# Further rows of each expert gathered as quarter rows and turned by one VectorE transpose, with a table of positions in 32-row blocks

## The chip, the core and the metric

The kernel runs on one core of a Trainium2 chip. The metric is the device time of one execution in microseconds (us), from three timed runs. A core has TensorE (PE in the profile, PEld for its weight loads), VectorE (DVE), ScalarE (ACT), GpSimd (POOL) and SyncE (SP, which here only issues DMAs). Each runs its own instruction stream in order; they meet at semaphores.

## The reference, cut to what matters

One decoder layer on 1024 tokens of width 1024: forgetting attention, layer norm, then a mixture of 64 experts of which each token picks 8, plus one shared expert, and a second layer norm. The part that matters here:

```python
scores = sigmoid(xf @ w_router); top_e = the 8 experts of a token; w = their weights
for each expert e, for the tokens that chose it:
    h  = silu(x @ w_gate[e]) * (x @ w_up[e])      # 1024 -> 256
    yb = (h @ w_down[e]) * w                       # 256 -> 1024
    acc[token] += yb
out = layer_norm(alpha * x + acc + shared(x))
```

How many tokens an expert gets depends on the data. The mean is 8 * 1024 / 64 = 128.

## The kernel before, in words

Attention takes the first part of the span. Then, tile by tile of 128 tokens, come the output projection, the first layer norm, the router, and `place`, in which VectorE works out for each of a token's 8 choices a slot in a table of positions in DRAM; POOL scatters the token numbers into it (`list_tokens`, eight indirect DMAs a tile, L635). The normed rows go to `rows_scratch` in DRAM, 1024 values and behind them the 64 routing weights, so that a row is 4352 bytes.

The expert stage runs the shared expert on eight tiles and then the 64 experts one after the other. Every expert takes its first 128 tokens as one block (POOL `gather`, L657: 128 whole rows into `x_rows`). If it has more, the rest goes in **further blocks** of 32 rows (`gather_further`, L670, into a buffer `x_rows2`). An expert has `nx` further blocks; on these inputs each has none or one.

TensorE works on 32-bit data as a high and a low part (`xb_hi`, `xb_lo` for rows, `gu_hi`, `gu_lo`, `dn_hi`, `dn_lo` for weights): ScalarE casts the high part, VectorE subtracts to get the low one. For each expert e, TensorE turns the hidden values of the expert before (`turn_h`, L1039), multiplies gate and up (`gate_up`, L1025, L1028, L1031), turns the rows of the next expert (`turn_next`, L1015), multiplies the expert before down (`down`, L1052 to L1060), and, if e has a further block, multiplies that (`gate_up_further`, L1084, L1085), whose 32 rows take high and low part side by side in `xo`. What is left of the further block is done one expert later: `turn_h_further` (L1093) and `down_further` (L1102, L1103).

The further block's rows have to be turned so that the width lies on the partitions. Before, TensorE does it in `turn_further` (L1074): eight transposes of 32 rows by 128 columns into half of a PSUM bank, between `turn_next` and `down`. ScalarE casts them to `xo` (`further_rows_hi`, L1486), VectorE subtracts (`further_rows_lo`, L1938), and TensorE's L1084 waits for that.

The order on VectorE within one expert is written out by hand in `expert` (L2008): low parts of weights (L1918), `h_of` (L1926), the last low part, `next_rows` (`xb_lo`, L1922, and the copy of the next expert's weights column, L1934), then, if the expert before had a further block, `further_y` (L1958), then `further_rows_lo` (L1938), then the low parts of the down weights. On POOL the order is: `gather` for the expert three ahead, `add_further`, `gather_further` for the expert two ahead, and `add_first` (L682), which adds a finished block into `sums_scratch` in DRAM. Each `add_first` waits until the one before has landed. POOL's instructions are strictly in this order, so what waits there holds up all that stands behind it.

The last expert's results don't go through DRAM but are placed by TensorE; the tiles are then summed, normed and stored.

Of the kernel before, what the change touches and what calls it, by code (L numbers as in the profile page):

```python
# [5 lines left out]
P = 128  # L6
BANK = 512
ALU = mybir.AluOpType
# [70 lines left out]
TAB_BLOCKS = 1 + (T - P) // XR  # L79
TAB = E * TAB_BLOCKS  # L80
ROWS = T + P
ROW_W = D + E
# [13 lines left out]
def build(nc, x, w_in, b_f, w_out, ln1_g, ln1_b, router, router_bias, w_gate, w_up, w_down, ws_gate, ws_up,  # L96
          ws_down, ln2_g, ln2_b, out):
    with ExitStack() as ctx:
# [18 lines left out]

        rows_dram = nc.dram_tensor("rows_scratch", (ROWS, ROW_W), F32, kind="Internal").ap()


        sums = [nc.dram_tensor(f"sums_scratch{i}", (ROWS, D), F32, kind="Internal").ap() for i in range(2)]
        tab_dram = nc.dram_tensor("tab_scratch", (P * TAB, 1), I32, kind="Internal").ap()
# [9 lines left out]
        with ExitStack() as early:  # L132
# [37 lines left out]
            with ExitStack() as d:  # L170
# [50 lines left out]
                pos_b = sb("pos_b", [P, E], c=d)  # L221
                pos_h = sb("pos_h", [P, E], c=d)
# [7 lines left out]
                tab0 = sb("tab0", [P, TAB], I32, c=d)  # L230
                zeros = sb("zeros", [P, ROW_W], c=d)
                nblk = [sb(f"nblk{i}", [1, E], c=d) for i in range(2)]
                nblk_i = [sb(f"nblk_i{i}", [1, E], I32, c=d) for i in range(2)]
        with ExitStack() as m:
# [3 lines left out]
            xg = [sb(f"x_rows{i}", [P, ROW_W], c=m) for i in range(3)]  # L238
# [4 lines left out]
            gu_x = sb("gu_x", [XR, 2 * FF], c=m)  # L243
# [8 lines left out]
            sidx = [sb(f"sidx{i}", [P, 1], I32, c=m) for i in range(3)]  # L252
            sb("to_64_bytes", [P, 8], c=m)
# [4 lines left out]
            tab = sb("tab", [P, TAB], I32, c=m)  # L258
# [121 lines left out]
        def _(sp):  # L380
# [89 lines left out]
            def tile(t):  # L470
# [4 lines left out]
                sp.dma_start(rows_dram[ds(t * P, P), 0:D], x1[:]).then_inc(S["x1_stored"], 16)  # L475
# [3 lines left out]
            def weights_out(t):  # L479
                sp.wait_ge(S["wts_ok"], t + 1)  # L480
                sp.dma_start(rows_dram[ds(t * P, P), D:ROW_W], wts[:]).then_inc(S["wts_stored"], 16)
# [30 lines left out]
            def load_rows(b):  # L512
                sp.dma_start(xg[b % 2][:, 0:D], rows_dram[b * P:(b + 1) * P, 0:D]).then_inc(rows_in[b % 2], 16)
# [32 lines left out]
            sp.wait_ge(S["c_fill"], 48)  # L546
            sp.wait_ge(S["extra_ok"], 2)
            sp.dma_start(tab[:], tab_dram.rearrange("(p n) o -> p (n o)", p=P)).then_inc(S["c_loads"], 16)
# [36 lines left out]
        def _(pool):  # L585
# [27 lines left out]
            g.iota(e8[:], pattern=[[TAB_BLOCKS, E]], base=1, channel_multiplier=0, allow_small_or_imprecise_dtypes=True).then_inc(S["c_const"], 1)  # L613
            g.iota(tok_all[:], pattern=[[P, TT]], base=0, channel_multiplier=1).then_inc(S["c_const"], 1)
            g.iota(tab0[:], pattern=[[0, TAB]], base=T, channel_multiplier=1).then_inc(S["c_const"], 1)
# [5 lines left out]
            pool.dma_start(tab_dram.rearrange("(p n) o -> p (n o)", p=P), tab0[:]).then_inc(S["c_fill"], 16)  # L621
            pool.dma_start(rows_dram[T:ROWS, :], zeros[:]).then_inc(S["c_fill"], 16)
            pool.dma_start(sums[0][T:ROWS, :], zeros[:, 0:D]).then_inc(S["c_fill"], 16)
            pool.dma_start(sums[1][T:ROWS, :], zeros[:, 0:D]).then_inc(sent[2], 16)
            pool.wait_ge(S["c_fill"], 48)
# [20 lines left out]
            def gather(i, e, count, free):  # L646


                if not (static(e) and e < 2):
                    pool.wait_ge(got[i], 8 * (e - i))  # L650
                stand(pool)
                g.tensor_copy(gidx[i][:], tab[:, ds(e * TAB_BLOCKS, 1)]).then_inc(idx_ok[i], 1)
                pool.wait_ge(idx_ok[i], count + 1)
                for s, value in free:
# [3 lines left out]
                                     in_offset=bass.IndirectOffsetOnAxis(ap=gidx[i][:, 0:1], axis=0)).then_inc(got[i], 16)  # L658

            def gather_further(par, e, k, x):  # L660

                if not static(x):
                    with pool.If(x > 0):
                        pool.wait_ge(S["x_in"], 16 * x)
# [1489 lines left out]
```

## Time and profile before

| what | value |
|---|---|
| three timed runs | 1650.76, 1644.61, 1645.97 us |
| their median | 1645.97 us |
| span of the profiled execution (first to last instruction) | 1640.5 us |
| median less that span | 5.5 us |
| PE busy, share of the span | 1578.0 us, 96% |
| DVE busy | 1182.3 us, 72% |
| ACT busy | 1032.5 us, 63% |
| POOL busy | 503.7 us, 31% |
| DMA, mean over the span | 225 GB/s |

The profile is one execution; of its time the records hold the span alone, and what lies around it is taken as the 5.5 us by which the median stands above it. A row of the timeline begins with the start and the duration in us; in square brackets stands how long the engine sat idle before it and who ended the wait. The profile's matmul durations overlap, since matmuls are pipelined: what one costs is read from start to start. A row of the groups has the line, engine, operation, tiles (out<-in), shapes and count, then busy us in total and mean ns of one, then idle us before and who ended it.

### The profile page before, as it was taken

How to read it: one execution, taken by the hardware profiler on the slowest of the kernel's cores; microseconds unless marked ns; L12 is line 12 of the kernel's file. 1: busy time of each engine (PE TensorE's matmuls, PEld its weight loads, DVE VectorE, ACT ScalarE, POOL GpSimd, SP SyncE). 2: the span in 40 equal slices, each digit the busy share in tenths (PEclk: the TensorE clock that was granted, in tenths of full speed). 3: DMA queues.
4: the chain of work that ended last, by engine and by line, in shares of the span. 5: the costliest groups of instructions: out<-in, count | busy, mean ns of one | idle time of the engine just before them, and what ended most of it. 6: DMA issues, size and time to landing. Idle time of an engine off the chain costs nothing.

```text
span 1640.5 us, 32188 instructions
## 1 busy us (share of the span) xinstructions
PE 1578.0 (96%) x8246; PEld 1310.0 (80%) x8247; DVE 1182.3 (72%) x2036; ACT 1032.5 (63%) x1706; POOL 503.7 (31%) x495
## 2 busy tenths in 40 slices
PE   6999999999999999899999999999999999999986
PEld 6897888888887788778878888888888888888863
DVE  4214777777777788847777787777876787888866
ACT  3214666666666655527677787666776777877854
POOL 0000000000000135432544454543454445454426
PEclk9999999999999999899999999999999999999995
DMA  7223222222123533657999999999999999999987
GB/s 245 91 81 91 72 48 68 58 65 71 45 71 103 170 134 138 227 196 281 337 291 318 305 357 367 326 289 264 334 318 288 274 353 331 342 368 370 367 252 282
DMA packets 161320, 368.63 MB, mean 225 GB/s; under 512 B 53009, under 2 KB 73489, under 8 KB 161265
## 3 DMA queue, kind: packets, MB, share of 16 engines
q1 hardware_dynamic: 136272, 284.21, 49.7%
q0 software_dynamic: 24992, 83.73, 19.7%
q8 instruction: 28, 0.46, 0.1%
q14 instruction: 28, 0.22, 0.0%
HBM read 294.39 MB, written 65.11 MB: 219 GB/s over the span
## 4 chain that ended last, share of the span: by engine, by line
PE 72%; DVE 8%; DMA 8%; issue 5%; ACT 3%; ACTq 2%; POOL 1%; SPq 0%; DVEq 0%; POOLq 0%
PE bank_pair L1025 6%; PE bank_pair L1031 6%; PE bank_pair L1028 6%; DMA sums_scratch<-ys,sidx 5%; PE q_ps L91 4%; PE q_ps L93 4%; PE q_ps L92 4%; PE out_ps L916 4%; PE k_ps L894 4%; PE out_ps L1084 3%; PE out_ps L1085 3%; PE q_ps L1015 3%; PE k_ps L1052 2%; PE k_ps L1053 2%; PE k_ps L1060 2%
## 5 line engine op out<-in xcount | busy, mean ns | idle before, releaser
L1918 DVE TENSOR_TENSOR gu_lo<-raw_gu,gu_hi 128x1024 fp32r<-128x1024 f32 x260 | 306.3, 1220 | 25.5 <-ACT gu_hi L1396 25.5
L1396 ACT CAST gu_hi<-raw_gu 128x1024 fp32r<-128x1024 f32 x260 | 253.2, 1050 | 2.3 <-DMA raw_gu<-in_moe_w_gate_dram 1.5
L1025 PE MATMUL bank_pair<-gu_hi,xb_hi 128*128 128x512 f32 x576 | 233.1, 405 | 5.5 <-DVE gu_lo L1918 4.2
L1028 PE MATMUL bank_pair<-gu_lo,xb_hi 128*128 128x512 f32 x576 | 226.9, 394 | 0.0
L682 POOL DMA_INDIRECT sums_scratch<-ys,sidx x63 | 122.1, 1939 | 148.9 <-DMA sums_scratch<-ys,sidx 116.0
L1918 DVE TENSOR_TENSOR dn_lo<-raw_dn,dn_hi 128x1024 fp32r<-128x1024 f32 x130 | 152.6, 1213 | 2.9 <-ACT dn_hi L1396 2.4
L1031 PE MATMUL bank_pair<-gu_hi,xb_lo 128*128 128x512 f32 x576 | 142.7, 390 | 2.0 <-DVE xb_lo L1922 2.0
L1301 ACT CAST pt_hi<-k_ps 128x512 fp32r<-128x512 f32 (+1 forms) x192 | 85.7, 482 | 75.4 <-PE k_ps L894 74.7
L1025 PEld LDWEIGHTS bank_pair<-gu_hi,xb_hi 128*128 128x128 f32 x576 | 110.1, 191 | 28.8 <-issue 6.4
L613 POOL IOTA e<- 128x64 f32 x1 | 0.2, 185 | 428.8 <-DVE xs L1714 428.8
L1396 ACT CAST dn_hi<-raw_dn 128x1024 fp32r<-128x1024 f32 x130 | 130.0, 1052 | 2.9 <-DMA raw_dn<-in_moe_w_down_dram 2.9
L1031 PEld LDWEIGHTS bank_pair<-gu_hi,xb_lo 128*128 128x128 f32 x576 | 108.0, 188 | 24.8 <-DVE xb_lo L1922 2.4
L1028 PEld LDWEIGHTS bank_pair<-gu_lo,xb_hi 128*128 128x128 f32 x576 | 109.7, 190 | 21.1
L657 POOL DMA_INDIRECT x_rows<-rows_scratch,gidx x64 | 77.4, 1210 | 154.2 <-DVE wcol L1934 122.6
L1692 DVE TENSOR_TENSOR pt_lo<-k_ps,pt_hi 128x512 fp32r<-128x512 f32 (+1 forms) x192 | 100.4, 551 | 27.8 <-ACT pt_hi L1301 27.0
L1052 PE MATMUL k_ps<-dn_hi,ht_hi 128*128 128x512 f32 x288 | 118.4, 411 | 0.0
L1053 PE MATMUL k_ps<-dn_lo,ht_hi 128*128 128x512 f32 x288 | 112.5, 391 | 0.0
L91 PE MATMUL q_ps<-xt_hi,wqk_hi 128*128 128x512 f32 x256 | 109.2, 427 | 0.0
L1290 ACT ACTIVATE probs<-bank_pair,nm 128x512 f32<-128x512 f32 (+3 forms) x128 | 74.7, 586 | 43.2 <-DVE nm L1685 29.7
L1084 PE MATMUL out_ps<-gu_hi,xo 128*128 128x512 f32 x248 | 97.3, 392 | 4.5 <-DVE xo L1938 4.5
L93 PE MATMUL q_ps<-xt_hi,wqk_lo 128*128 128x512 f32 x256 | 100.5, 393 | 0.0
L92 PE MATMUL q_ps<-xt_lo,wqk_hi 128*128 128x512 f32 x256 | 100.3, 392 | 0.0
(306 smaller groups left out, 3973.7 us busy)
## 6 DMA issues: line engine op xcount, KB each, us to landing
raw_gu<-in_moe_w_gate_dram SPq DMA_DIRECT2D x128, 512.0 KB, 6.8
raw_gu<-in_moe_w_up_dram SPq DMA_DIRECT2D x128, 512.0 KB, 8.6
raw_dn<-in_moe_w_down_dram SPq DMA_DIRECT2D x128, 512.0 KB, 8.3
wqk<-in_fox_w_in_dram SPq DMA_DIRECT2D x66, 128.0 KB, 2.5
v_scratch<-v_out SPq DMA_DIRECT2D x32, 256.0 KB, 2.8
va<-v_scratch SPq DMA_DIRECT2D x16, 512.0 KB, 4.7
fin<-sums_scratch SPq DMA_DIRECT2D x16, 512.0 KB, 8.3
xs<-in_x_dram SPq DMA_DIRECT2D x8, 512.0 KB, 7.4
```

The source lines that it names most:

```text
L91: pe.matmul(out, w_hi, m_hi, start=start, stop=False, skip_group_check=True)
L92: pe.matmul(out, w_hi, m_lo, start=False, stop=False, skip_group_check=True)
L93: return pe.matmul(out, w_lo, m_hi, start=False, stop=stop, skip_group_check=True)
L682: g.indirect_dma_start(out=sums[0], out_offset=bass.IndirectOffsetOnAxis(ap=sidx[par][:, 0:1], axis=0), in_=ys[par][:], in_offset=None, co ...
L1025: i = pe.matmul(o3, xb_hi[s][:, c], g_hi[:, :, c], start=c == 0, stop=False, skip_group_check=True)
L1028: pe.matmul(o3, xb_hi[s][:, c], g_lo[:, :, c], start=False, stop=False, skip_group_check=True)
L1031: i = pe.matmul(o3, xb_lo[s][:, c], g_hi[:, :, c], start=False, stop=c == DC - 1, skip_group_check=True)
L1052: pe.matmul(k_ps[:, r], ht_hi[:, c], d_hi[:, c, r], start=c == 0, stop=False, skip_group_check=True)
L1053: pe.matmul(k_ps[:, r], ht_hi[:, c], d_lo[:, c, r], start=False, stop=False, skip_group_check=True)
L1084: pe.matmul(o3, xo[:, c], g_hi[:, :, c], start=c == 0, stop=False, skip_group_check=True)
L1396: a.copy(hi, raw).then_inc(S[done], 1)
L1918: dve.tensor_tensor(lo, raw, hi, ALU.subtract).then_inc(S[lo_ok], 1)
```

## The change

Further rows are no longer gathered as 32 whole rows. `rows_scratch` is read as quarter rows of 256 values, and one indirect DMA brings 128 quarter rows: partition 32q + r gets quarter q of row r (`x_quarters`). A single VectorE transpose, which turns squares of 32 by 32, then gives `xq_t` in the layout that the eight TensorE transposes gave. It reads the 256 values of a partition with a step of 8 values (`"p (k c) -> p c k"`). The turn stands on VectorE between the last low part of the gate and up weights and `next_rows`; TensorE's `turn_further` and its wait are gone. `xo` is made from `xq_t` in SBUF where it was made from PSUM.

For the quarters POOL needs four times the row number plus the quarter (`qidx`), one more instruction on POOL, and the routing weights lie in a DRAM tensor of their own, so that both the first gather and the further one are followed by a second indirect DMA for the weights (`w_rows`, `w_further`). The table of positions is laid out in blocks of 32 rows, which takes three of `place`'s VectorE instructions out, and is loaded by eight DMAs where one did. `gu_x` has 128 partitions, of which 96 stay zero, and `turn_h_further` turns 128 columns.

```diff
@@ gather, on POOL
                 g.indirect_dma_start(out=xg[i][:], out_offset=None, in_=rows_dram,
                                      in_offset=bass.IndirectOffsetOnAxis(ap=gidx[i][:, 0:1], axis=0)).then_inc(got[i], 16)
+                g.indirect_dma_start(out=wg[i][:], out_offset=None, in_=wts_dram,
+                                     in_offset=bass.IndirectOffsetOnAxis(ap=gidx[i][:, 0:1], axis=0)).then_inc(got[i], 16)
@@ gather_further, on POOL
-                g.tensor_copy(gidx[2][0:XR], tab[0:XR, ds(e * TAB_BLOCKS + k + 1, 1)]).then_inc(idx_ok[2], 1)
-                pool.wait_ge(idx_ok[2], x + 1)
+                g.tensor_copy(gidx[2][:], tab_more[:, ds(k * E + (e + E), 1)]).then_inc(idx_ok[2], 1)
+                pool.wait_ge(idx_ok[2], 2 * x + (QUARTERS + 1))
                 stand(pool)
-                g.indirect_dma_start(out=xg[2][par * XR:(par + 1) * XR], out_offset=None, in_=rows_dram,
+                g.tensor_scalar(qidx[:], gidx[2][:], float(QUARTERS), quarter_of[:, 0:1], ALU.mult, ALU.add).then_inc(idx_ok[2], 1)
+                g.indirect_dma_start(out=wx[par][:], out_offset=None, in_=wts_dram,
                                      in_offset=bass.IndirectOffsetOnAxis(ap=gidx[2][0:XR, 0:1], axis=0)).then_inc(S["x_in"], 16)
+                pool.wait_ge(idx_ok[2], 2 * x + (QUARTERS + 2))
+                stand(pool)
+                g.indirect_dma_start(out=xq[par][:], out_offset=None, in_=quarters_dram,
+                                     in_offset=bass.IndirectOffsetOnAxis(ap=qidx[:, 0:1], axis=0)).then_inc(S["x_in"], 16)
@@ on TensorE
-            def turn_further(par, x):
-                pe.wait_ge(S["x_in"], 16 * x + 16)
...
-                    i = pe.transpose(banks[1][:, FF + c * XR:FF + (c + 1) * XR], v[:, c], ident[rows, rows])
...
-                    i = pe.transpose(out_ps[:, c * XR:(c + 1) * XR], v[:, c], ident[0:XR, 0:XR])
+                    i = pe.transpose(out_ps[:, c * P:(c + 1) * P], v[:, c], ident[:])
...
-                    pe.wait_ge(S["ht_lo_ok"], m)
-                    turn_further(par, xi + nx - 1)
                     down(m - 1, par, e + 1)
@@ on VectorE
+            def turn_further(par, x):
+                dve.wait_ge(S["x_in"], 32 * x + 32)
+                stand(dve)
+                dve.transpose(xq_t[:], xq[par][:].rearrange("p (k c) -> p c k", c=DC)).then_inc(S["x_turned"], 1)
...
                     next_weights(range(G_PIECES - 1, G_PIECES))
+                    with dve.If(nx > 0):
+                        turn_further(par, xi)
                     next_rows()
@@ place, on VectorE
-                dve.scalar_tensor_tensor(out=pos_h[:], in0=pos_q[:], scalar=float(P // XR), in1=pos_q[:], op0=ALU.is_lt, op1=ALU.mult)
-                step(dve.tensor_scalar(pos_b[:], pos_q[:], float(1 - P // XR), 0.0, ALU.add, ALU.max))
-                step(dve.tensor_tensor(pos_b[:], pos_b[:], e8[:], ALU.add))
-                step(dve.scalar_tensor_tensor(out=dest[:], in0=pos_m[:], scalar=float(TAB), in1=pos_b[:], op0=ALU.mult, op1=ALU.add))
-                step(dve.scalar_tensor_tensor(out=dest[:], in0=pos_h[:], scalar=float(XR * TAB), in1=dest[:], op0=ALU.mult, op1=ALU.add))
+                step(dve.scalar_tensor_tensor(out=dest[:], in0=pos_q[:], scalar=float(E), in1=e8[:], op0=ALU.mult, op1=ALU.add))
+                step(dve.scalar_tensor_tensor(out=dest[:], in0=pos_m[:], scalar=float(TAB), in1=dest[:], op0=ALU.mult, op1=ALU.add))
```

Three places show what moves. The first is TensorE within an expert that has one further block, from the end of `down_further` to the further block's first matmuls. Before:

```order
L1103 MATMUL out_ps<-dn_lo,ho 128x512
L1193 ISA
L1193 COMPARE_AND_BRANCH
L1192 UNCONDITIONAL_BRANCH
L1199 REGISTER_ALU
L1069 ISA
L1074 MATMUL bank_pair<-ident,x_rows 128x32 x8
L1047 REGISTER_ALU
L1049 REGISTER_ALU
L1052 MATMUL k_ps<-dn_hi,ht_hi 128x512
```

And now, with the lines of the changed file:

```order
L1119 MATMUL out_ps<-dn_lo,ho 128x512
L1209 ISA
L1209 COMPARE_AND_BRANCH
L1208 UNCONDITIONAL_BRANCH
L1072 REGISTER_ALU
L1073 REGISTER_ALU
L1075 REGISTER_ALU
L1078 MATMUL k_ps<-dn_hi,ht_hi 128x512
```

The eight transposes are gone, and nothing stands in their place. The second place is VectorE in an expert whose predecessor had a further block, from `h_of` to `further_y`. Before:

```order
L1926 TENSOR_TENSOR hh<-sg,bank_pair 128x256
L1917 REGISTER_ALU
L1918 TENSOR_TENSOR gu_lo<-raw_gu,gu_hi 128x1024
L1921 REGISTER_ALU
L1922 TENSOR_TENSOR xb_lo<-q_ps,xb_hi 128x1024
L1934 ISA
L1934 COPY wcol<-x_rows 128x1
L1958 TENSOR_TENSOR ys<-out_ps,ys 32x1024
```

And now:

```order
L1936 TENSOR_TENSOR hh<-sg,bank_pair 128x256
L1927 REGISTER_ALU
L1928 TENSOR_TENSOR gu_lo<-raw_gu,gu_hi 128x1024
L2053 REGISTER_ALU
L2053 COMPARE_AND_BRANCH
L1948 ISA
L1950 STREAM_TRANSPOSE xq_t<-x_quarters 128x256
L2053 UNCONDITIONAL_BRANCH
L1931 REGISTER_ALU
L1932 TENSOR_TENSOR xb_lo<-q_ps,xb_hi 128x1024
L1944 ISA
L1944 COPY wcol<-w_rows 128x1
```

The transpose has come in ahead of `xb_lo`, behind a branch on `nx`. The third place is POOL's further gather. Before:

```order
L667 COPY gidx<-tab 32x1
L668 REGISTER_ALU
L670 DMA x_rows<-rows_scratch,gidx 32x1088
```

And now:

```order
L685 COPY gidx<-tab_more 128x1
L686 ISA
L688 TENSOR_SCALAR qidx<-gidx,quarter_of 128x1
L689 DMA w_further<-wts_scratch,gidx 32x64
L691 REGISTER_ALU
L693 DMA x_quarters<-rows_scratch,qidx 128x256
```

One instruction and one indirect DMA have come in ahead of the rows' own gather, and a wait between them.

## Rows read from the trace of the kernel before

**Rows 1.** The page's table of engines: busy us, share, instructions.
```profile
PE 1578.0 (96%) x8246; PEld 1310.0 (80%) x8247; DVE 1182.3 (72%) x2036; ACT 1032.5 (63%) x1706; POOL 503.7 (31%) x495
```

**Rows 2.** Busy by stretch: length, then PE, PEld, DVE, ACT, POOL busy, clock, DMA.
```profile
1057.00:1141.00 84.00, 84.00 (x408) 68.51 (x407) 60.13 (x80) 55.65 (x76) 36.95 (x40) 1.00 0.94 287
```

**Rows 3.** Groups by line and shape, TensorE, 650 to 1600 us.
```profile
L1074 PE MATMUL bank_pair<-ident,x_rows 32*128 32x32 f32 x248 | 32.9, 272 | 0.4 <-DVE ht_lo L1930 0.4
L1039 PE MATMUL bank_pair<-ident,hh 128*128 128x128 f32 x144 | 29.0, 283 | 1.5 <-DVE hh L1926 0.9 <-DVE base L1863 0.6
L1093 PE MATMUL out_ps<-ident,gu_x 32*128 32x32 f32 x62 | 13.0, 289 | 0.9 <-DVE gu_x L1948 0.9
```

**Rows 4.** Timeline of an expert whose predecessor had no further block, 1005 to 1011.
```profile
1006.44 1.06 PE L1074 MATMUL bank_pair<-ident,x_rows 32*128 32x32 f32 x8
1007.43 0.50 PE L1052 MATMUL k_ps<-dn_hi,ht_hi 128*128 128x512 f32 x1
...
1008.79 0.41 DVE L1938 TENSOR_TENSOR xo<-bank_pair,xo 128x256 fp32r<-128x256 f32 x1
...
1010.29 0.39 PE L1084 MATMUL out_ps<-gu_hi,xo 128*128 128x512 f32 x1
```

**Rows 5.** Timeline of another such expert, 1053 to 1054.
```profile
1053.32 0.41 DVE L1938 TENSOR_TENSOR xo<-bank_pair,xo 128x256 fp32r<-128x256 f32 x1
...
1053.78 0.50 PE L1084 MATMUL out_ps<-gu_hi,xo 128*128 128x512 f32 x1 [0.86 <-DVE xo L1938]
```

**Rows 6.** Line L1938: who waited for it, us in total, times.
```profile
  PE out_ps L1084: 4.5, 6
```

**Rows 7.** Line L1074: what ended TensorE's idle time before it, us, times.
```profile
  issue: 6.3, 16
```

**Rows 8.** Timeline of an expert whose predecessor had a further block, TensorE and VectorE.
```profile
1067.67 0.50 PE L1052 MATMUL k_ps<-dn_hi,ht_hi 128*128 128x512 f32 x1
...
1070.52 0.39 PE L1084 MATMUL out_ps<-gu_hi,xo 128*128 128x512 f32 x1
...
1067.91 1.21 DVE L1958 TENSOR_TENSOR ys<-out_ps,ys 32x1024 f32<-32x1024 f32 x1 [0.65 <-ACT ys L1504]
1069.05 0.40 DVE L1938 TENSOR_TENSOR xo<-bank_pair,xo 128x256 fp32r<-128x256 f32 x1
```

**Rows 9.** Groups by line and shape, VectorE, 650 to 1640 us.
```profile
L1922 DVE TENSOR_TENSOR xb_lo<-q_ps,xb_hi 128x1024 fp32r<-128x1024 f32 x72 | 88.0, 1222 | 8.9 <-ACT xb_hi L1424 7.5
...
L1930 DVE TENSOR_TENSOR ht_lo<-bank_pair,ht_hi 128x256 fp32r<-128x256 f32 x72 | 29.6, 411 | 36.4 <-ACT ht_hi L1432 36.4
...
L1948 DVE SCALAR_TENSOR_TENSOR gu_x<-gu_x,w_x 32x256 f32<-32x256 f32 x31 | 14.7, 476 | 4.7 <-ACT gu_x L1495 4.7
```

**Rows 10.** Groups by line and shape, POOL, 650 to 1640 us.
```profile
L682 POOL DMA_INDIRECT sums_scratch<-ys,sidx x63 | 122.1, 1939 | 148.9 <-DMA sums_scratch<-ys,sidx 116.0 <-POOL sidx L677 21.8 <-issue 11.2
L657 POOL DMA_INDIRECT x_rows<-rows_scratch,gidx x64 | 77.4, 1210 | 154.2 <-DVE wcol L1934 122.6 <-POOL gidx L652 28.6 <-issue 3.0
...
L652 POOL COPY gidx<-tab 128x1 int32 x58 | 29.7, 512 | 49.4 <-issue 49.0
```

**Rows 11.** Timeline of POOL: one row at 1084, two at 1460 to 1468.
```profile
1084.68 1.00 POOL L657 DMA_INDIRECT x_rows<-rows_scratch,gidx  x1 [5.21 <-DVE wcol L1934]
...
1460.11 1.85 POOL L682 DMA_INDIRECT sums_scratch<-ys,sidx  x1 [2.42 <-DMA sums_scratch<-ys,sidx]
...
1466.87 1.00 POOL L657 DMA_INDIRECT x_rows<-rows_scratch,gidx  x1 [3.61 <-DVE wcol L1934]
```

**Rows 12.** The chain that ended last: first and last of ten rows between these.
```profile
1501.34 9.86 DMA sums_scratch<-ys,sidx
...
1592.45 6.13 DMA sums_scratch<-ys,sidx
```

**Rows 13.** Groups by line and shape, VectorE, two of the instructions of `place`.
```profile
L1870 DVE TENSOR_TENSOR pos_b<-pos_b,e 128x64 f32<-128x64 f32 x8 | 1.8, 226 | 0.3
...
L1869 DVE TENSOR_SCALAR pos_b<-pos_q 128x64 f32<-128x64 int32 x8 | 1.5, 188 | 0.0
```

More of the change, by code:

```diff
@@ L252, in build @@
             sidx = [sb(f"sidx{i}", [P, 1], I32, c=m) for i in range(3)]
+            qidx = sb("qidx", [P, 1], I32, c=m)
+            quarter_of = sb("quarter_of", [P, 1], c=m)
             sb("to_64_bytes", [P, 8], c=m)
@@ L545, in _ @@
             sp.wait_ge(S["listed"], 16 * TT * TOP_K)
-            sp.wait_ge(S["c_fill"], 48)
+            sp.wait_ge(S["c_fill"], 64)
             sp.wait_ge(S["extra_ok"], 2)
-            sp.dma_start(tab[:], tab_dram.rearrange("(p n) o -> p (n o)", p=P)).then_inc(S["c_loads"], 16)
+            table = tab_dram.rearrange("(p n) o -> p (n o)", p=XR)
+            for a in range(FIRST_BLOCKS):
+                sp.dma_start(tab_first[a * XR:(a + 1) * XR], table[:, a * E:(a + 1) * E]).then_inc(S["c_loads"], 16)
+            for a in range(QUARTERS):
+                sp.dma_start(tab_more[a * XR:(a + 1) * XR, E:], table[:, FIRST_BLOCKS * E:]).then_inc(S["c_loads"], 16)
             next_gate_up(3, 1)
@@ L711, in _ @@
                     pool.dma_start(sums[0][(b - 1) * P:b * P, :], ys[(b - 1) % 2][:]).then_inc(sent[(b - 1) % 2], 16)
+            for q in range(QUARTERS):
+                g.memset(quarter_of[q * XR:(q + 1) * XR], float(q)).then_inc(idx_ok[2], 1)
+            pool.wait_ge(idx_ok[2], QUARTERS)
             gather(0, 2, 1, [(S["w_ok"], 1)])
@@ L1065, in down @@
                 down_lo(b, w)
-            def turn_further(par, x):
-                pe.wait_ge(S["x_in"], 16 * x + 16)
-                stand(pe)
-                rows = slice(par * XR, (par + 1) * XR)
-                v = strided(xg[2][rows, 0:D])
-                for c in range(DC):
-                    i = pe.transpose(banks[1][:, FF + c * XR:FF + (c + 1) * XR], v[:, c], ident[rows, rows])
-                i.then_inc(S["x_turned"], 1)
             def gate_up_further(w, x):
@@ L1512, in load_counts @@
             def load_counts(e):
-                return [act.value_load(earlier[0:1, ds(e + k, 1)], min_val=0, max_val=E * TAB_BLOCKS) for k in range(4)]
+                return [act.value_load(earlier[0:1, ds(e + k, 1)], min_val=0, max_val=E * MORE) for k in range(4)]
             def expert(e, par, pos, counts):
@@ L2004, in load_counts @@
             def load_counts(e):
-                return [dve.value_load(earlier[0:1, ds(e + k, 1)], min_val=0, max_val=E * TAB_BLOCKS) for k in range(4)]
+                return [dve.value_load(earlier[0:1, ds(e + k, 1)], min_val=0, max_val=E * MORE) for k in range(4)]
             def expert(e, par, counts, last=False):
@@ L2054, in expert @@
                         further_y(xi + k)
+                        turn_further(par, xi + k + 1)
                     further_rows_lo(par, e, after - 1)
```

128 lines of the change are left out of this document (71 added, 57 removed).

## The prediction

> **What bounds the kernel now.** I read the table of engines first: TensorE is busy for 96% of the span, VectorE for 72%, POOL for 31% [rows 1]. Then the busy time by stretch: in 84 us of the expert stage TensorE is busy without a gap, at full clock, while VectorE has work for 69 us and POOL for 37 [rows 2]. So the expert stage is as long as TensorE's instructions are, and a microsecond taken out of TensorE's stream there shortens the kernel, as long as TensorE does not stand waiting for something instead. POOL's 31% says less than it seems to: it works in strict order and waits for its own DMAs, so it can be full without being busy.
>
> Then the groups of the line that goes, and what it waits for. L1074 has 248 rows, eight to a block: 31 further blocks [rows 3]. Of the 31, 16 begin with idle time that nothing in the profile explains ("issue", 0.39 us each) [rows 7]; 15 of these are the experts whose predecessor had a further block too (call them **B**), the 16th is the last expert. The other 15 have a predecessor without one (**A**).
>
> **What the removal gives, by what TensorE meets next.** The next instruction that needs the rows is L1084, which waits for `xo`. Taking the turn out can bring L1084 forward only to the moment at which `xo` is there.
>
> In a usual A the turn takes TensorE from 1006.44 to 1007.43, 0.99 us. `xo` is finished at 1008.79 + 0.41 = 1009.20, and L1084 starts at 1010.29 [rows 4]: 1.09 us to spare. Where L1084 does wait, it starts 0.05 us after `xo` is done (1053.73 to 1053.78) [rows 5], so 1.04 us can be had. But VectorE's transpose (of length T) now stands ahead of `next_rows` and so ahead of `further_rows_lo`, with no wait between them in a usual A to hide it: `xo` comes T later than it did. Gain: 1.04 − T.
>
> In six A's TensorE waits for `xo` already, 4.5 us in all [rows 6], as at 1053.78. There the removal only makes the wait longer, and T is a plain loss: −T.
>
> In a B, `xo` is done at 1069.05 + 0.40 = 1069.45 and L1084 starts at 1070.52; less the 0.05 and rounded down 0.99 us is to be had, which is also all of the turn [rows 8]. VectorE waits 0.65 us for ScalarE's `ys` before `further_y` [rows 8], which the new transpose fills: `further_y`, and `xo` behind it, start when they did. Gain: 0.99, less what T has over 0.65.
>
> Of the 15 A's, seven are usual ones, six late, and two lie between with about 0.3 us to spare and are entered as nothing. The last expert's turn, too, is entered as nothing, since the chain of adds [rows 12] ends after it. So the gain is G(T) = 15 × 0.99 + 7 × (1.04 − T) − 6T = 22.1 − 13T up to T = 0.65, and above that 28T falls off in place of 13T.
>
> **T.** No VectorE transpose is in the trace, nor a read that steps by 8 values. From below the nearest row is 0.19 us (64 values, L1869) [rows 13], from above 1.22 us (1024 values, `xb_lo`) [rows 9]. Rows with 256 values a partition are 0.41 (one operand in PSUM) and 0.48 (both in SBUF) [rows 9]. I take 0.48, since the work is 256 values a partition in SBUF. Then G = 15 × 0.99 + 7 × 0.56 − 6 × 0.48 = 14.9 + 3.9 − 2.9 = **15.9 us**. At 0.19 it is 19.6; at 1.22 it is 15 × 0.42 − 7 × 0.18 − 6 × 1.22 = −2.3, a small loss.
>
> **`turn_h_further` with 128 columns.** The two transposes of 32 x 32 cost 289 ns each in the records, those of 128 x 128 of L1039 283 [rows 3]. Entered as nothing: the same number of instructions at the same price.
>
> **`place`.** Three instructions go: two of 128 x 64 with two operands, like L1870 at 0.226, and one at 0.188 (L1869) [rows 13]; 0.64 us a tile, 5.1 over eight tiles. VectorE is on the path there for only part of the tiles; I enter **2 us**, bounds 0 and 5.
>
> **POOL.** Each expert gets a second indirect gather behind the first; a further block gets one too, and a small arithmetic instruction with a wait for it. An indirect gather occupies POOL for 1.21 us (L657), the small instruction 0.51 (L652), the wait for its result 28.6 / 64 = 0.45 [rows 10]. For two experts with one further block between them that is 3 × 1.21 + 0.51 + 0.45 = 4.6 us. In such a pair POOL has 2.42 + 3.61 = 6.0 us in which it waits for others; in a B it is 5.21 before one gather [rows 11]. A gain of 15.9 over 32 pairs takes 0.5 of it. So it fits, with 0.9 to spare, and is entered as nothing. What is queued behind the new gathers is `add_first`, and behind that the next `gather`, whose rows TensorE needs an expert later. If this cover is gone, every microsecond over the idle time is one on the kernel.
>
> **The end.** The chain that ended last is, from 1501 us on, ten landings of `add_first`, each waiting for the one before, from 9.86 us at the first to 6.13 at the last [rows 12]. There the end is not set by TensorE. What TensorE gains in these 94 of some 900 us, about 1.6, does not reach the end; and the new gathers stand between the adds on POOL's instruction stream and go through the same DMAs. From nothing to one gather each, 10 × 1.21 = 12 us; nearest is a fifth of that, since POOL can issue the gather while an add is in flight: 2.4. Together **4 us** of loss.
>
> Table loads, fills and `quarter_of` lie ahead of or beside the shared expert and are entered as nothing.
>
> **The sum.** 1640.5 − 15.9 − 2 + 4 = 1626.6 for the span; with the 5.5 us around it **1632 us**, against a median of 1646.
>
> **The rivals.**
>
> *The step of 8 slows the transpose.* If the transpose takes two passes' worth, 2 × 0.41 = 0.82 us, then G = 15 × (0.99 − 0.17) + 7 × 0.22 − 6 × 0.82 = 12.3 + 1.5 − 4.9 = 8.9, and the time is 1640.5 − 8.9 − 2 + 4 + 5.5 = 1639. For it: no row reads by steps, and squares must be filled before they can be emptied. Against: VectorE's rows go by values per partition whatever the operand (0.41 and 0.48 for two sources). The Trainium skill speaks against this change here: "Vector Engine (DVE) Microarchitecture Reference", section 5.2, states that a stream keeps its full rate only where neighbouring words come in pairs, and gives 1.73 to 2.50 ns a column where every element hops, against 1.04 in order, with some 75 ns per instruction; for 256 columns that is an estimate of 0.52 to 0.72 us, by which the sum would gain 15.4 to 11.7. No row of this trace shows it.
>
> *The adds swallow it.* If each of the ten adds at the end is later by a whole gather, the loss there is 12 + 1.6 in place of 4: 1642. For it: in 116.0 of `add_first`'s 148.9 us of idle time it waits for its own earlier DMA [rows 10], so delays there add up. Against: the gather occupies POOL while the DMA before is in flight.
>
> *POOL becomes the bound (the slower case).* If an added indirect DMA takes POOL as long as `add_first` does, 1.94 us [rows 10], in place of 1.21, a pair has 3 × 1.94 + 0.96 = 6.8 us more for 6.0 of idle time, and with some 31 pairs the kernel is 31 × 0.75 = 23 us longer and gains nothing on TensorE: 1640.5 + 23 − 2 + 5.5 = 1667. It decides from (6.0 − 0.96) / 3 = 1.7 us per added DMA on; at 1.8 it is 1654. For it: the margin is small. Against: the gathers of the trace, of 128 rows of 4352 bytes, cost 1.21 in the mean, and only the adds cost 1.94.
>
> *The wait takes the turn's place.* TensorE would then stand before L1084 for as long as it turned. This is T above 1.04 + 0.1, where G is nothing, 1648; it lies in the first rival's tail.
>
> **How the numbers follow.** The forecast (T from 0.4 to 0.55, adds nearly hidden) gets 0.50, the slow step 0.20 (the tail included), the adds 0.18, POOL 0.12. Half a per cent, 8.2 us, is about what a measurement of this kernel tells from no change: faster means below 1637.7, slower above 1654.2. The forecast's own range: T = 0.19, adds' chain unchanged and 4 for `place` give 1640.5 − 19.6 − 4 + 5.5 = 1622; T = 0.55, 8 for the adds and 0 for `place` give 1640.5 − 15 + 8 + 5.5 = 1639. Nearly all of it is faster: 0.48. Of the slow step 0.06 is faster, 0.13 the same, 0.01 slower; of the adds 0.06, 0.11 and 0.01; of POOL 0.02 is the same and 0.10 slower. Together 0.60, 0.26 and 0.12, with the 0.02 left of the forecast in the same band. The range 1624 to 1648 holds the forecast but its lower edge, the slow step up to a G of nothing, and the adds; it leaves out POOL.
>
> **What the changed profile would show.** No TensorE transposes between `turn_next` and `down`, and 31 VectorE transposes at about 480 ns: 800 would be the first rival. L1084's counterpart waits for `xo` in the six late A's for T + 1 us longer each, and nearly nowhere else. VectorE's 0.65 us before `further_y` is gone in the B's. POOL has two groups of weight gathers at about 1.2 us, and its idle time is shorter, but TensorE waits nowhere for rows. If TensorE idles before `turn_next` for gathered rows, POOL has become the bound. At the end the same ten adds; if their steps are a microsecond longer, the second rival holds. I am wrong as to the mechanism if TensorE's waits for `xo` come to more than the 31 us that the turns took, or if the transpose waits on VectorE for quarter rows that have not landed, and with it all that VectorE does for the next expert.

## The result, and the profile after

The changed kernel takes 1871.17 us (median; 1866.57 to 1874.23) where the kernel before takes 1646.53: 1.1364 times as long, with a 95% interval of 1.1338 to 1.139. The forecast was 1632. In the profiled execution (1873.41 us, a span of 1871.7) TensorE is idle far more; the page's table of engines, which answers to [rows 1]:

```profile
PE 1594.4 (85%) x7998; PEld 1316.4 (70%) x7999; DVE 1188.3 (63%) x2044; ACT 1032.1 (55%) x1706; POOL 687.2 (37%) x626
```

TensorE's work is there as it was but for the 248 turns (it is busy for 16 us more, some of it at a lower clock), with 277 us of idle time in place of 62. Where it is idle the busy time by stretch shows: from the first entry into the table of positions to the shared expert's first matmul, then to the first routed expert, then to the end of the last expert's gate and up. A row has the stretch and its length; then PE, PEld, DVE, ACT, POOL busy; clock; DMA share; GB/s. After:

```profile
596.00:775.60 179.60, 81.13 (x352) 67.06 (x350) 60.36 (x212) 36.91 (x48) 43.15 (x44) 0.69 0.83 59
775.60:937.80 162.20, 90.83 (x385) 73.61 (x385) 47.48 (x143) 32.47 (x44) 33.90 (x39) 0.77 0.81 105
937.80:1806.70 868.90, 804.95 (x3697) 658.51 (x3696) 661.90 (x842) 607.08 (x782) 563.96 (x497) 0.96 0.96 310
```

The same three stretches before:

```profile
596.00:670.20 74.20, 67.31 (x344) 55.83 (x343) 62.35 (x223) 36.29 (x48) 42.37 (x44) 0.94 0.41 142
670.20:754.00 83.80, 80.22 (x385) 66.65 (x385) 48.93 (x151) 32.68 (x44) 30.65 (x37) 0.95 0.57 203
754.00:1577.70 823.70, 814.06 (x3936) 670.74 (x3936) 650.20 (x809) 606.58 (x780) 385.11 (x370) 1.00 0.99 327
```

The reader is to see two losses. The routing, where the engines do the same work as before, takes 105 us longer up to the shared expert and 78 more beside it, 184 in all, and the DMA engines are busy for 0.8 of that time while they move 59 GB/s where they moved 142, and beside the shared expert 105 where they moved 203. The expert stage takes 45 us longer, with 9 us less TensorE work and 179 us more of POOL.

What the routing waits for is the line that scatters token numbers into the table. Who waited for it, after (us in total, times):

```profile
  POOL tok L647: 202.6, 7
  DVE dest_i L1888: 159.8, 7
```

and before:

```profile
  POOL tok L631: 22.4, 7
  DVE dest_i L1878: 4.4, 2
```

The chain that ended last, after, holds seven such landings (start, us); the first and the last of them:

```profile
605.50 32.47 DMA tab_scratch<-tok,dest_i
...
845.05 33.65 DMA tab_scratch<-tok,dest_i
```

The first tile's eight scatters are issued from 596.18 on and have landed at 605.50 + 32.47 = 637.97: 41.8 us for 1024 numbers of 4 bytes, 41 ns each in the mean. The six tiles after it take 36.0 to 42.6 us each. Before, a scatter landed 2.4 us (median) after its issue.

In the expert stage the groups of POOL, after (line, operation, tiles, count; busy us, mean ns; idle us before):

```profile
L675 POOL DMA_INDIRECT w_rows<-wts_scratch,gidx x62 | 93.4, 1507 | 18.9 <-issue 18.9
L673 POOL DMA_INDIRECT x_rows<-rows_scratch,gidx x62 | 87.2, 1406 | 68.7 <-POOL gidx L668 45.6 <-DVE wcol L1944 23.0
...
L693 POOL DMA_INDIRECT x_quarters<-rows_scratch,qidx x31 | 42.6, 1374 | 9.5 <-issue 9.5
...
L689 POOL DMA_INDIRECT w_further<-wts_scratch,gidx x31 | 40.2, 1297 | 12.5 <-POOL qidx L688 11.2 <-issue 1.3
...
L688 POOL TENSOR_SCALAR qidx<-gidx,quarter_of 128x1 int32<-128x1 int32 x31 | 28.5, 920 | 6.9 <-POOL gidx L685 6.0 <-issue 0.9
```

Against [rows 10], the time in which a gather waits for VectorE has gone from 122.6 to 23.0 us: POOL has little left to wait for. TensorE's largest wait there, and VectorE's new transpose, after:

```profile
PE out_ps L1100 <- DVE xo L1954: 40.7, 13, 8.2
```

```profile
L1950 DVE STREAM_TRANSPOSE xq_t<-x_quarters 128x256 f32<-128x256 f32 x31 | 20.5, 662 | 5.3 <-DMA x_quarters<-rows_scratch,qidx 5.3
```

### The profile page after: what moved, and what is told of

It is laid out like the page before. It is cut to its first block, busy times and chain, and to the rows that moved or that the text cites. A ratio compares the mean times of both kernels' runs of the same rounds, so it can differ in the third digit from the quotient of the medians.

```text
span 1871.7 us, 32037 instructions
## 1 busy us (share of the span) xinstructions
PE 1594.4 (85%) x7998; PEld 1316.4 (70%) x7999; DVE 1188.3 (63%) x2044; ACT 1032.1 (55%) x1706; POOL 687.2 (37%) x626
## 4 chain that ended last, share of the span: by engine, by line
PE 32%; DMA 23%; POOL 16%; issue 15%; POOLq 7%; DVE 4%; ACT 2%; DVEq 1%; SPq 0%; ACTq 0%
DMA tab_scratch<-tok,dest_i 11%; DMA sums_scratch<-ys,sidx 9%; POOLq L722 4%; PE out_ps L942 3%; PE q_ps L95 3%; PE q_ps L96 3%; PE q_ps L97 3%; POOL tab_scratch L651 3%; PE k_ps L920 3%; POOL x_quarters L693 2%; POOL sidx L700 2%; DMA sums_scratch<-ys 2%; POOL w_rows L675 1%; POOL gidx L668 1%; POOL qidx L688 1%
## 5 line engine op out<-in xcount | busy, mean ns | idle before, releaser
L1051 PE MATMUL bank_pair<-gu_hi,xb_hi 128*128 128x512 f32 x576 | 237.8, 413 | 4.8 <-DVE gu_lo L1928 3.1
L1057 PE MATMUL bank_pair<-gu_hi,xb_lo 128*128 128x512 f32 x576 | 147.6, 399 | 34.7 <-DVE xb_lo L1932 34.7
L1057 PEld LDWEIGHTS bank_pair<-gu_hi,xb_lo 128*128 128x128 f32 x576 | 110.2, 192 | 59.7 <-DVE xb_lo L1932 35.5
L705 POOL DMA_INDIRECT sums_scratch<-ys,sidx x63 | 115.3, 1830 | 99.0 <-DMA sums_scratch<-ys,sidx 50.2
L1100 PE MATMUL out_ps<-gu_hi,xo 128*128 128x512 f32 x248 | 110.4, 445 | 46.7 <-DVE xo L1954 40.7
L673 POOL DMA_INDIRECT x_rows<-rows_scratch,gidx x64 | 90.2, 1409 | 70.4 <-POOL gidx L668 47.4
L1101 PE MATMUL out_ps<-gu_lo,xo 128*128 128x512 f32 x248 | 106.5, 430 | 0.0
L675 POOL DMA_INDIRECT w_rows<-wts_scratch,gidx x64 | 96.4, 1506 | 19.5 <-issue 19.5
```

The lines of the kernel that those rows point to most:

```text
L675: g.indirect_dma_start(out=wg[i][:], out_offset=None, in_=wts_dram, in_offset=bass.IndirectOffsetOnAxis(ap=gidx[i][:, 0:1], axis=0)).then_ ...
L705: g.indirect_dma_start(out=sums[0], out_offset=bass.IndirectOffsetOnAxis(ap=sidx[par][:, 0:1], axis=0), in_=ys[par][:], in_offset=None, co ...
L1051: i = pe.matmul(o3, xb_hi[s][:, c], g_hi[:, :, c], start=c == 0, stop=False, skip_group_check=True)
L1057: i = pe.matmul(o3, xb_lo[s][:, c], g_hi[:, :, c], start=False, stop=c == DC - 1, skip_group_check=True)
L1100: pe.matmul(o3, xo[:, c], g_hi[:, :, c], start=c == 0, stop=False, skip_group_check=True)
L1101: i = pe.matmul(o3, xo[:, c], g_lo[:, :, c], start=False, stop=c == DC - 1, skip_group_check=True)
```

## The experiments

The theories after the result. **Table:** the new layout's addresses make the scatter slow and cost all 184 us ahead of the experts; its rivals are the distance between the table's rows alone, and something else in the routing. **POOL:** the added gathers fill POOL, and the expert stage waits for it; its rival is that the quarter rows (128 pieces where 32 went) or the transpose make the stalls. **Late rows:** with POOL free, what is lost is where `xo` comes late.

All results in one place. "First expert" is the start of its first matmul, "experts" goes from there to the same instruction of the last expert (the expectations count some 4 us more, to the end of the last one's gate and up), "rest" from there to the end; all from the timeline of the one profiled execution. That of before (a span of 1640.5 us) and that of e_units (1612.36 us) are faster than the other executions of their kernels, and the first expert comes at 754.0 before and at 759.1 and 759.5 in two kernels with the same table, so that a few us in that column say nothing.

| kernel | time, us | ratio to before (95%) | first expert | experts | rest |
|---|---|---|---|---|---|
| before | 1646.53 | | 754.0 | 820.0 | 66.5 |
| changed | 1871.17 | 1.1364 (1.1338 to 1.139) | 937.8 | 865.2 | 68.7 |
| e_table_alone | 1844.82 | one run | 958.1 | 822.1 | 63.0 |
| e_padrow | 1688.90 | one run | 761.6 | 857.2 | 68.4 |
| e_pad16 | 1721.73 | one run | 793.0 | 860.7 | 66.2 |
| e_pad1024 | 1732.98 | one run | 801.0 | 861.7 | 68.5 |
| e_spread | 1688.39 | 1.0231 (1.0201 to 1.0261) | 759.5 | 860.9 | 66.4 |
| e_before_gathers | 1656.11 | one run | 759.1 | 830.0 | 65.4 |
| e_before_pool | 1674.65 | one run | 759.5 | 847.6 | 65.8 |
| e_onegather | 1642.60 | 0.9963 (0.9948 to 0.9979) | 759.8 | 818.4 | 62.6 |
| e_contig | 1641.04 | one run | 759.9 | 814.0 | 65.4 |
| e_early | 1618.21 | 0.9811 (0.9795 to 0.9828) | 760.0 | 797.3 | 59.7 |
| e_units | 1619.30 | 0.9827 (0.9811 to 0.9843) | 752.7 | 796.2 | 61.8 |

On the chips of the experiments the kernel before took 1649.08, 1648.32 and 1648.94 us.

**e_table_alone** puts the changed table into the kernel before:

```diff
-                step(dve.tensor_tensor(pos_b[:], pos_b[:], e8[:], ALU.add))
...
+                step(dve.scalar_tensor_tensor(out=dest[:], in0=pos_q[:], scalar=float(E), in1=e8[:], op0=ALU.mult, op1=ALU.add))
+                step(dve.scalar_tensor_tensor(out=dest[:], in0=pos_m[:], scalar=float(TAB), in1=dest[:], op0=ALU.mult, op1=ALU.add))
```

> The kernel before, with the new table alone (layout, place, loads); rows, gathers and turns are those of before. If the table's layout is what costs, TensorE's first gate and up of the shared expert starts about 105 us later and the first expert about 184 us later than before, and the time is about 1830. If the loss ahead of the experts comes from something else of the change (weights in a tensor of their own, the fills), the time is 1640 to 1650.

The first expert comes 204 us later than before and the expert stage is what it was (822.1 against 820.0): the table alone carries the loss ahead of the experts, and none of the one in the expert stage. It is 20 us more than in the changed kernel; POOL's waits for the landings are longer by as much (223.2 against 202.6 us), and why no run shows:

```profile
POOL tok L638 <- DMA tab_scratch<-tok,dest_i: 223.2, 7, 34.4
```

**e_padrow, e_pad16, e_pad1024** change one number, the distance between the table's rows in DRAM:

```diff
+ROW = TAB + 64
...
-        tab_dram = nc.dram_tensor("tab_scratch", (XR * TAB, 1), I32, kind="Internal").ap()
+        tab_dram = nc.dram_tensor("tab_scratch", (XR * ROW, 1), I32, kind="Internal").ap()
```

(16 and 1024 in the other two, with `place`, fill and loads to match.)

> The changed kernel, with each of the table's 32 rows in DRAM 64 words longer (8448 bytes in place of 8192); experts still lie side by side, one word apart. If the scatter is slow because the table's rows stand a power of two apart, the eight scatters of a tile land some 12 us after the first is issued (they take 42 now) and the time falls by about 184 us, to 1690. If it is slow because the slots of all 64 experts of one position share 256 bytes, nothing changes: 1866 to 1875, the eight scatters still 42 us.

> The changed kernel, with each of the table's rows in DRAM 16 words longer (8256 bytes in place of 8192), where 64 words longer cured it. Sixteen rows of a tile then cover 16 x 64 bytes and the 256 behind them in place of one and the same 256 bytes, counted modulo 8192. If what costs is the writes' falling on the same addresses modulo 8192, this cures most of it: eight scatters in 12 to 20 us, time 1690 to 1740. If the rows must lie 256 bytes or more apart modulo 8192 for it, the time stays above 1800.

> The changed kernel, with rows of the table 1024 words longer (12288 bytes): modulo 8192 the rows fall on two places of 256 bytes in turn. If addresses count modulo 8192, the writes are served at twice the speed: the eight scatters of a tile take some 21 us in place of 42 and the time is 1720 to 1790. If any larger power of two is as good as 8192, and 4096 too, it stays near 1870; if only a distance of 8192 is bad, it is 1690.

The waits of POOL for the landings, of e_padrow, e_pad16 and e_pad1024 in turn:

```profile
POOL tok L648 <- DMA tab_scratch<-tok,dest_i: 25.7, 7, 6.1
```

```profile
POOL tok L648 <- DMA tab_scratch<-tok,dest_i: 71.2, 7, 12.7
```

```profile
POOL tok L648 <- DMA tab_scratch<-tok,dest_i: 80.1, 7, 13.3
```

All three times lie in the ranges that the account by addresses had. With 64 words the wait is that of the kernel before; experts still lie side by side in 256 bytes, so that these neighbours alone are not the cause.

**e_spread** keeps rows 8192 bytes apart and spreads the experts over them:

```diff
-                step(dve.scalar_tensor_tensor(out=dest[:], in0=pos_q[:], scalar=float(E), in1=e8[:], op0=ALU.mult, op1=ALU.add))
+                step(dve.scalar_tensor_tensor(out=dest[:], in0=pos_q[:], scalar=1.0, in1=e8[:], op0=ALU.mult, op1=ALU.add))
...
+                        dve.tensor_copy(blocks(q)[:, :, 0:1], blocks(0)[:, :, q:q + 1]).then_inc(S["c_loads"], 16)
```

> The changed kernel, with the slots of neighbouring experts 128 bytes apart in DRAM in place of 4 (expert times 32 plus block); the table is loaded once and copied to the other three partition groups by six VectorE copies. Rows of the table still stand 8192 bytes apart. If shared 256 bytes are what costs, the eight scatters land within 12 us and the time is 1871 - 184 = 1687 (1680 to 1700), with the expert stage still at 869 us. If the row distance costs, the time stays near 1870.

```profile
POOL tok L643 <- DMA tab_scratch<-tok,dest_i: 17.1, 7, 6.1
```

That cures it as well (the line above is the same wait, of e_spread), so that the distance of 8192 bytes alone is not the cause either. Each of my two single causes predicted one of the two cures wrongly. What holds in all five is both together. An expert gets 16 of a tile's tokens on average, so the first tile's 1024 numbers go to the first 16 rows and some behind them, at the same 256 bytes of each; later tiles reach into the 256 bytes beside them too. The rows lie 8192 apart, so that counted modulo 8192 a tile falls into a few hundred bytes. Padding moves the rows apart, spreading widens the piece, and 1024 words leave two places, which halves the 41.8 us to 10.3 of issues and at most 13.3 of wait. Since 12288 is a multiple of 4096, agreeing modulo 4096 is not enough; a larger power of two than 8192 would fit the halving as well, and no run rules it out. Nor does the time go by the number of 256-byte places: 16 words of padding spread the first tile over some 1280 bytes, five such places, and a tile takes 18.3 to 23.2 us there, as long as with two places (19.8 to 23.7). How large a piece the writes must share to be slow stays open. The expert stage stays 37 to 42 us longer than before in all four cures.

**e_onegather** is e_spread with weights ahead of their rows again (64 + 1024 values), and reads a quarter as 320 values:

```diff
-                g.indirect_dma_start(out=wg[i][:], out_offset=None, in_=wts_dram,
-                                     in_offset=bass.IndirectOffsetOnAxis(ap=gidx[i][:, 0:1], axis=0)).then_inc(got[i], 16)
...
-                g.indirect_dma_start(out=wx[par][:], out_offset=None, in_=wts_dram,
...
-                g.indirect_dma_start(out=xq[par][:], out_offset=None, in_=quarters_dram,
+                g.indirect_dma_start(out=xq[par][:], out_offset=None, in_=units_dram,
```

> As the spread table, and the weights stand ahead of their row again (64 + 1024 values), so that the first gather brings them; a quarter is read as 320 values, so that the first quarter brings the further rows' weights. Both weight gathers are gone from POOL; quarter rows, the VectorE transpose and one more small instruction on POOL stay. If POOL's added gathers cause the stalls of the expert stage, that stage falls from 869 us to some 808 to 815 (before: 824) and the time to about 1632 (1625 to 1640). If the quarter rows themselves (128 descriptors of 1 KB, landing late) cause them, the stage stays above 850 and the time above 1670.

The stage falls by 42 us, to 818.4; the quarter rows and the transpose are still there, so without the weight gathers the quarter rows and the transpose make no such loss. The time is 10 us above what I expected, a miss that the later runs take up.

**e_before_gathers and e_before_pool** go the other way: the kernel before with the unused weight gathers, and then with the small instruction too:

```diff
+                g.indirect_dma_start(out=wg[i][:], out_offset=None, in_=wts_dram,
+                                     in_offset=bass.IndirectOffsetOnAxis(ap=gidx[i][:, 0:1], axis=0)).then_inc(got[i], 16)
...
+                g.tensor_scalar(qidx[0:XR], gidx[2][0:XR], 4.0, 0.0, ALU.mult, ALU.add).then_inc(idx_ok[2], 1)
+                pool.wait_ge(idx_ok[2], 2 * x + 2)
```

> The kernel before, with one more indirect gather of 64 weights behind each gather and each further gather; nothing uses what they bring, but the rows count as there only with them. If POOL's instruction stream has no room for them, the expert stage grows from 824 us by 20 to 45 us and TensorE waits for rows, hidden values or sums in places where it did not: 1668 to 1692. If POOL has room, and the stalls need the quarter rows or the transpose, 1645 to 1655.

> The kernel before with the unused weight gathers, and in each further gather the changed kernel's small POOL instruction and the wait for it. With the gathers alone the expert stage grew by 10 us. If POOL's own time is what counts, another 31 x 1.4 us on it bring the stage to 20 to 35 us above before and the time to 1665 to 1685. If the changed kernel's stalls came from its 128 quarter rows, the stage stays at some 10 us more and the time at 1650 to 1660.

The first was a miss: 10 us more in the expert stage, not 20 to 45. POOL still had room there; gathers waited for VectorE for 44.5 us in it:

```profile
POOL x_rows L662 <- DVE wcol L1943: 44.5, 14, 6.4
```

With the small instruction and its wait the stage is 27.6 us longer, as POOL's time has it, with no quarter row and no transpose in the kernel. So it is not one of the added steps but their sum that runs over. The changed kernel loses 18 us more; the room is smaller there, which I take for the reason but no run separates, since TensorE's stretch for an expert with a further block behind another is 15.4 us there and 16.6 in these.

**e_contig** reads the quarter rows in order, which puts the further rows' values into `xq_t` in another order and makes the sums others than the layer's; only its times are read:

```diff
-                dve.transpose(xq_t[:], xq[par][:, E:].rearrange("p (k c) -> p c k", c=DC)).then_inc(S["x_turned"], 1)
+                dve.transpose(xq_t[:], xq[par][:, E:].rearrange("p (c k) -> p c k", c=DC)).then_inc(S["x_turned"], 1)
```

> As the version with one gather, but the transpose reads the 256 values of a partition one after the other in place of every eighth, so the further rows' values come in another order (part of the computation is changed by that). If the step of 8 is what makes it 0.66 us, it takes 0.3 to 0.45 us now and the time falls by some 2 us; if a transpose of 128 x 256 costs two passes in any order, it stays at 0.62 to 0.68 us.

Its group of transposes:

```profile
L1941 DVE STREAM_TRANSPOSE xq_t<-x_quarters 128x256 f32<-128x256 f32 x31 | 13.6, 438 | 0.0
```

The step of 8 costs 0.22 us of the 0.66; the 0.44 that is left is what other instructions with 256 values a partition take (0.41 to 0.48 [rows 9]), so that a second pass is not there. The time moved by 1.6 us, which says nothing beside a spread of 7 us in e_onegather's ten runs.

**e_early** changes the order on VectorE in experts whose predecessor had no further block (`only_rows_lo` is `further_rows_lo` in an expert with one further block):

```diff
                     next_weights(range(G_PIECES - 1))
+                    with dve.If(nx > 0):
+                        turn_further(par, xi)
...
                     h_of(m)
+                    only_rows_lo()
                     next_weights(range(G_PIECES - 1, G_PIECES))
-                    with dve.If(nx > 0):
-                        turn_further(par, xi)
                     next_rows()
```

> As the version with one gather, and in experts whose predecessor had no further block VectorE turns the quarter rows before h_of, 1.6 us earlier, and makes the low part of the further rows before the last low part of the weights and next_rows, some 2 us earlier. If these experts are slow because xo is late behind xb_lo, and TensorE then runs at half clock after the wait, its waits for xo fall from 28 us in 16 places to under 12, the stretches of 17.5 us become about 14, and the time falls by 8 to 14 us, to 1628 to 1634. If the quarter rows have not landed by then, VectorE waits for them and nothing is won: 1640 or more.

TensorE's wait for `xo` falls from 28.3 to 10.3 us, the time by 24 us, more than I expected, since the usual A's gain too. Of e_onegather, and then of e_early:

```profile
PE out_ps L1091 <- DVE xo L1945: 28.3, 16, 5.9
```

```profile
PE out_ps L1091 <- DVE xo L1945: 10.3, 7, 5.5
```

**e_units** takes the small instruction off POOL (and gives the further blocks' sums rows of 1088 values in DRAM, so that the same addresses serve for them):

```diff
-                dve.tensor_copy(blocks(q)[:, :, FIRST_BLOCKS:], blocks(0)[:, :, FIRST_BLOCKS:]).then_inc(S["c_loads"], 16)
+                dve.tensor_scalar(blocks(q)[:, :, FIRST_BLOCKS:], blocks(0)[:, :, FIRST_BLOCKS:], float(UNITS), float(q * (QW // E)), ALU.mult, ALU.add).then_inc(S["c_loads"], 16)
```

> As the version with the early turn, and the table of further rows holds ready-made addresses (17 times the row plus 4 times the quarter, made once by VectorE), so that POOL has no more instructions and waits than before the change. If the stall that is left near the start (23.0 us where others take 15.4) and the small ones come from POOL being late with add_further, they go and the time is 5 to 9 us below that with the early turn. If they come from the transfers themselves (128 pieces where 32 went), nothing changes.

A miss in the time: 1619.30 against 1618.21, the same. The stretch of 23.0 us near the start is 15.6 in its profile, as expected if POOL was late with `add_further`, but the expert stage is only 1.1 us shorter: most other stretches are 0.1 to 0.25 us longer. At a granted clock of 1.00 in both, 14 matmuls take 3.21 us in e_early and 3.28 in e_units, 0.229 and 0.234 apart, and so all through the stage:

```profile
1490.73 0.39 PE L1045 MATMUL bank_pair<-gu_lo,xb_hi 128*128 128x512 f32 x1
...
1493.94 0.39 PE L1045 MATMUL bank_pair<-gu_lo,xb_hi 128*128 128x512 f32 x1
```

```profile
1484.13 0.39 PE L1043 MATMUL bank_pair<-gu_lo,xb_hi 128*128 128x512 f32 x1
...
1487.41 0.40 PE L1043 MATMUL bank_pair<-gu_lo,xb_hi 128*128 128x512 f32 x1
```

Why its matmuls are slower no run shows. e_early is the version to take: 0.9811 of before.

## Why the prediction was wrong, point by point

**`place`, entered as a gain of 2 us: the step that failed.** I priced the table by the VectorE instructions that its new layout saves, with bounds of 0 and 5, and by its loads, and never the scatter that writes it, though its addresses are what the layout changes. Measured: +184 us before the first expert, +204 for the table alone. The 2 us themselves can't be seen beside that; they stay open.

**POOL, entered as nothing: the second step that failed.** The rival "POOL becomes the bound" was right in kind. The sum for a pair of experts with a further block was 4.6 us, against 6.0 in which POOL waited. An added DMA took 1.51 + 0.30 of gap (18.9 / 62) = 1.81 behind the first gather and 1.30 behind the further one, in place of 1.21; the small instruction took 0.92 where I had 0.51, and the gap behind it, mostly the wait for its result, 12.5 / 31 = 0.40 where I had 0.45. That is 2 × 1.81 + 1.30 + 0.92 + 0.40 = 6.2 us: more than that idle time. In a run of experts with further blocks, 49 us long, no other engine and no DMA is named any more in POOL's waits. The longest of them (engine, line, waited for: us, times, longest):

```profile
POOL gidx L668 <- issue: 4.9, 4, 1.6
POOL sums_scratch L705 <- issue: 2.9, 3, 1.0
POOL x_rows L673 <- POOL gidx L668: 2.6, 3, 0.9
```

and before, a like run, where it waits for VectorE and for an add too:

```profile
POOL x_rows L657 <- DVE wcol L1934: 4.1, 1, 4.1
...
POOL sums_scratch L682 <- DMA sums_scratch<-ys,sidx: 3.0, 1, 3.0
```

The path to TensorE was another than the one I gave, too. I had the gathered rows come late, to be seen ahead of `turn_next`; there TensorE waited once, for 0.2 us. What came late is `add_further`, which stands on POOL behind the first gather and its added weights: only when it has landed is the buffer `ys` free, into which ScalarE copies the next further block's result; VectorE's `further_y` waits for that copy, `xo` stands behind it, and TensorE waits for `xo`. After, in the longest of these:

```profile
1455.41 1.39 POOL L715 DMA_INDIRECT sums_scratch<-ys,sidx  x1 [0.97 <-POOL sidx L711]
1462.33 1.00 ACT L1516 COPY ys<-out_ps 32x1024 f32<-32x1024 f32 x1 [9.10 <-DMA sums_scratch<-ys,sidx]
1463.37 1.21 DVE L1973 TENSOR_TENSOR ys<-out_ps,ys 32x1024 f32<-32x1024 f32 x1 [8.20 <-ACT ys L1516]
```

TensorE then waits 8.2 us before L1100. ScalarE waits so in five places:

```profile
ACT ys L1516 <- DMA sums_scratch<-ys,sidx: 28.4, 5, 9.1
```

Before, it nowhere does; in e_before_pool it does in four, for 21.0 us, in e_onegather in one, for 6.8. So my own sign for this rival would have missed it, and the sign against the mechanism came true: TensorE's waits for `xo` are 40.7 us, more than 31.

Of the 63 distances from one expert to the next, 18 are longer by more than 0.45 us, 61 us in all, and the others are shorter by 16 together: 45. Four of them, in which TensorE waited 5.2 to 8.2 us and then ran at half clock for some 6, make 29 of the 61.

**The gain on TensorE was right where nothing stood in the way.** In eight of the 15 B's the stretch of an expert went from 16.6 to 15.4 or 15.5 us (forecast 0.99 of gain), and the other seven were held up; in the usual A's it went from 14.2 to 13.8 (forecast 1.04 − T = 0.38 with the T measured). The two A's between, entered as nothing, lost 0.4 each.

**T** was 0.66 us, not 0.48, between the forecast and the first rival. By the figures of the Trainium skill's "Vector Engine (DVE) Microarchitecture Reference", section 5.2, measured there on other operations, the estimate was 0.52 to 0.72 for a read that hops at every element: the trace agrees with 0.66. For a read in order the same figures give an estimate of 256 × 1.04 + 75 ns = 0.34 us; e_contig's 0.44 lies above it.

**The six late A's were mis-sized.** I had −T each; in five of them the stretch went from some 15.3 to 17.4 us, 2.1 more. T is 0.66 of that; the rest is the clock. In e_onegather TensorE waits 2.80 us for `xo` in such an expert, whose stretch is 17.7 us, and the matmuls behind start 0.43 us apart (0.24 again at the end) for some 3 us:

```profile
1178.26 0.50 PE L1091 MATMUL out_ps<-gu_hi,xo 128*128 128x512 f32 x1 [2.80 <-DVE xo L1945]
...
1179.98 0.63 PE L1092 MATMUL out_ps<-gu_lo,xo 128*128 128x512 f32 x1
1180.41 0.63 PE L1091 MATMUL out_ps<-gu_hi,xo 128*128 128x512 f32 x1
...
1182.70 0.40 PE L1091 MATMUL out_ps<-gu_hi,xo 128*128 128x512 f32 x1
1182.94 0.40 PE L1092 MATMUL out_ps<-gu_lo,xo 128*128 128x512 f32 x1
```

The stretches around it (columns as above; the clock is the third from the end):

```profile
1172.00:1178.00 6.00, 3.46 (x19) 2.60 (x17) 6.00 (x9) 4.45 (x8) 4.18 (x4) 1.00 1.03 345
1178.00:1184.00 6.00, 5.74 (x19) 4.63 (x20) 2.56 (x4) 2.22 (x4) 2.80 (x3) 0.72 1.04 357
```

A mean of 0.72 is some 3 us at half speed (1.2 GHz) among full. The same run shows what is left without it: in another late A TensorE waits 2.52 us, goes on at full clock, and the stretch is 15.9 us.

```profile
1374.43 0.50 PE L1091 MATMUL out_ps<-gu_hi,xo 128*128 128x512 f32 x1 [2.52 <-DVE xo L1945]
```

```profile
1374.00:1380.00 6.00, 5.57 (x25) 4.67 (x26) 3.68 (x7) 3.44 (x6) 3.88 (x3) 1.00 1.02 349
```

So the half clock costs 1.6 to 1.9 us where it comes, and the length of the wait alone doesn't tell whether it comes: a third one, of 2.53 us, ends in a stretch of 17.5. Before, TensorE waited 0.86 us [rows 5] and went on at full speed. The turn had one more use than I saw: it kept TensorE busy while `xo` was made. With the order of e_early the six stretches are 13.8 to 15.1 us and the usual A's 13.1, so that nearly the whole turn is gained there.

**The adds at the end, 4 us,** cost 2 (66.5 to 68.7). **128-column turns at nothing:** they cost 278 ns each, where those of 32 columns cost 289. **Loads and fills at nothing:** no run speaks against it.

## What to carry to other kernels

When a layout in DRAM changes, price the writes into it as well as the arithmetic that finds the place: list where the pieces of one scatter fall, and look twice at rows a power of two apart with the live part of each row small (8192 bytes here). An engine that works in strict order is full when it no longer waits for others, whatever its busy share says; count its instructions, gaps and waits for itself against the shortest stretch it must keep up with, which the change may shorten, and follow each of its transfers to what waits for its landing, freed buffers too. Work that looks removable on the busiest engine may be covering a wait: look at what the engine meets next, and move that forward in the same change.

## What was not expected of the hardware

Scattered writes of 4 bytes took 41 ns each in the mean when the addresses of a tile fell into a few hundred bytes modulo 8192, and its eight scatters landed at the pace of their issue with rows 8448 bytes apart, or with experts 128 bytes apart; which part of the memory does this no run shows. After waits of 2.53 and 2.80 us TensorE ran at half clock for some 3 us, after one of 2.52 it did not. And what I took for 5.5 us around the span is 1.7 in the runs that list both (1873.41 against 1871.7): the rest was the spread between executions, up to 8 us for the kernel before (1644.46 to 1652.79 over 13 runs).
